# Two output tiles of a weight piece computed together, contraction tile by contraction tile

## What is computed

```python
h = rmsnorm(x)
q_a, k_a, v_a, u_pool, q_mem = split(h @ w_in)
y0 = window_attention(q_a, k_a, v_a)        # 8 heads, window of two chunks of 64, ALiBi, sinks
y1 = multiscale_pool(u_pool)                # windows 2, 4, 8, 16, then a linear map per group
y2 = memory_attention(q_mem, mem_k, mem_v)  # 4 heads of 128 into 256 memory tokens
merged = sum(sigmoid(h @ Wg_i + bg_i) * (y_i @ w_branch_i) for i in range(3))
x = x + merged @ w_out
x = x + square(relu(rmsnorm(x) @ w_up)) @ w_down
out = rmsnorm(x)
```

## Time and profile before

| | |
|---|---|
| Time, median of 3 runs | 3052.1 us (3051.82 to 3055.05) |
| Span of the profiled execution (its own time, first to last instruction) | 3050.7 us |
| TensorE busy | 3000.1 us, 98% |
| VectorE busy | 1367.5 us, 45% |
| ScalarE busy | 982.3 us, 32% |
| GpSimd busy | 194.1 us, 6% |
| HBM traffic | 96 GB/s over the span |
| Mean granted TensorE clock | 0.996 |

### The profile page before, as it was taken

One profiled execution on the slowest core, in us unless ns is written; L12 is line 12 of the kernel. 1 busy time (PEld: TensorE's weight loads), 2 busy tenths in 40 slices (PEclk: granted clock), 3 DMA queues, 4 the chain that ended last, 5 costly groups with the idle time before them and its releaser, 6 DMA issues.

```text
span 3050.7 us, 36914 instructions
## 1 busy us (share of the span) xinstructions
PE 3000.1 (98%) x14045; PEld 2468.1 (81%) x14045; DVE 1367.5 (45%) x1709; ACT 982.3 (32%) x1457; POOL 194.1 (6%) x191
## 2 busy tenths in 40 slices
PE   8999999999999999999999999999999999999998
PEld 7788888888778888888877888888887788888886
DVE  4542354444344335544435424544444532454444
ACT  4442232222344233222234423322223432332223
POOL 0100110000010111000001011100000101100000
PEclk9999999999999999999999999999999999999999
DMA  5122333322312233333231224233322122432322
GB/s 187 35 78 85 118 131 97 97 96 97 98 39 90 90 124 118 97 97 100 93 98 39 83 90 164 84 102 97 97 91 84 51 82 97 160 97 92 98 97 86
DMA packets 290351, 294.06 MB, mean 96 GB/s; under 512 B 9704, under 2 KB 285212, under 8 KB 290204
## 3 DMA queue, kind: packets, MB, share of 16 engines
q1 hardware_dynamic: 287900, 283.71, 28.8%
q0 software_dynamic: 2304, 8.39, 0.7%
HBM read 283.67 MB, written 8.39 MB: 96 GB/s over the span
## 4 chain that ended last, share of the span: by engine, by line
PE 90%; issue 5%; DVE 2%; POOL 1%; ACT 1%; DMA 0%; POOLq 0%; DVEq 0%; ACTq 0%
PE ps L979 28%; PE ps L981 27%; PE ps L980 27%; PE ps L984 2%; PE ps L1108 2%; PE ps L1109 2%; PE ps L1077 1%; POOL sq_sum L957 1%; PE ps L1135 1%; PE ps L1118 1%; ACT sq L351 0%; DVE u_lo L792 0%; DVE scores L700 0%; DVE mx L705 0%; DVE out_tm L883 0%
## 5 line engine op out<-in xcount | busy, mean ns | idle before, releaser
L979 PE MATMUL ps<-h_hi,w_hi 128*128 128x512 f32 x2240 | 884.8, 395 | 12.5 <-issue 12.5
L980 PE MATMUL ps<-h_lo,w_hi 128*128 128x512 f32 x2240 | 874.6, 390 | 0.0
L981 PE MATMUL ps<-h_hi,w_lo 128*128 128x512 f32 x2240 | 874.6, 390 | 0.0
L611 DVE TENSOR_TENSOR w_lo<-stage,w_hi 128x2048 fp32r<-128x2048 f32 (+1 forms) x269 | 559.9, 2081 | 643.2 <-ACT w_hi L351 642.0
L351 ACT ACTIVATE w_hi<-stage 128x2048 fp32r<-128x2048 f32 (+2 forms) x287 | 485.1, 1693 | 525.7 <-PE ps L981 524.5
L979 PE MATMUL ps<-u_hi,w_hi 128*128 128x512 f32 x1280 | 501.5, 392 | 5.5 <-DVE u_lo L792 5.5
L979 PEld LDWEIGHTS ps<-h_hi,w_hi 128*128 128x128 f32 x2240 | 422.1, 188 | 100.6 <-issue 14.2
L981 PE MATMUL ps<-u_hi,w_lo 128*128 128x512 f32 x1280 | 498.8, 390 | 0.0
L980 PE MATMUL ps<-u_lo,w_hi 128*128 128x512 f32 x1280 | 498.4, 389 | 0.0
L981 PEld LDWEIGHTS ps<-h_hi,w_lo 128*128 128x128 f32 x2240 | 421.9, 188 | 88.1
L980 PEld LDWEIGHTS ps<-h_lo,w_hi 128*128 128x128 f32 x2240 | 422.1, 188 | 86.4 <-issue 1.0
(11 more groups left out here) (154 smaller groups left out, 2081.9 us busy)
## 6 DMA issues: line engine op xcount, KB each, us to landing
stage<-in_w_up SPq DMA_DIRECT2D x128, 512.0 KB, 4.6
stage<-in_w_down SPq DMA_DIRECT2D x128, 512.0 KB, 4.0
stage<-in_w_gate SPq DMA_DIRECT2D x96, 512.0 KB, 4.2
stage<-in_w_in SPq DMA_DIRECT2D x60, 512.0 KB, 4.7
stage<-in_w_out SPq DMA_DIRECT2D x32, 512.0 KB, 4.1
x_tm<-in_x SPq DMA_DIRECT2D x5, 2048.0 KB, 9.5
stage<-in_w_branch_attn SPq DMA_DIRECT2D x32, 256.0 KB, 3.0
stage<-in_w_branch_pool SPq DMA_DIRECT2D x32, 256.0 KB, 3.0
```

What stands on the lines that cost most here:

```text
L611: v.tensor_tensor(w_lo[:, slot, 0:kt, :], stage[:, slot, 0:kt, :], w_hi[:, slot, 0:kt, :].bitcast(F32), ALU.subtract).then_inc(lo_done, 1)
L979: mm(dst, wh, xh, start=first, stop=False)
L980: mm(dst, wh, xl, start=False, stop=False)
L981: return mm(dst, wl, xh, start=False, stop=last)
```

## The change

A new helper, `gemm_pair`, takes both tiles of a piece: for each contraction tile k it does the three matmuls of z = 0 in one bank, and then those of z = 1 in the next bank. `piece` waits for both banks first, and then calls it. The merge loop and the MLP use it too, apart from the first up piece of a block's first chunk, which stays as it was. In the attention stage the two groups of transposes move from k = 4 and 5 of the second tile to k = 6 and 7 of the pair. Each tile still signals `tile_done` with its last matmul.

```diff
+                def gemm_pair(slot, bank, xh, xl, kt=KT, ready=None, between=None):
+
+                    for k in range(kt):
+                        if ready is not None:
+                            ready(k)
+                        if between is not None:
+                            between(k)
+                        for z in range(2):
+                            wh, wl = w_hi[:, slot, k, z * P:(z + 1) * P], w_lo[:, slot, k, z * P:(z + 1) * P]
+                            last = product(ring[:, (bank + z) % 4, :], wh, wl, xh[:, k, :], xl[:, k, :], k == 0, k == kt - 1)
+                            if k == kt - 1:
+                                last.then_inc(tile_done, 1)
+
                 def piece(n, q0, xh, xl, kt=KT, ready=None, between=None):
 
                     pe.wait_ge(lo_done, p0 + (n + 1))
                     for z in range(2):
                         q = q0 + z
                         pe.wait_ge(emptied[q % 4], e0 + q // 4)
-                        gemm(n % 2, z, q % 4, xh, xl, kt, between if z else ready)
+                    gemm_pair(n % 2, q0 % 4, xh, xl, kt, ready, between)
...
-                        f = k - 4
+                        f = k - 6
...
                         for z in range(2):
                             bank = (2 * r + z) % 4
                             pe.wait_ge(emptied[bank], ej + r // 2)
-                            gemm(r % 2, z, bank, xh, xl, kt)
+                        gemm_pair(r % 2, (2 * r) % 4, xh, xl, kt)
...
-                            for z in range(2):
+
+                            def rows_done(k):
+                                if half and i == 0:
+                                    pe.wait_ge(u_lo_done, uc + (k + 1))
+
+                            if not (first and half == i == 0):
+                                q = place(8 * half + 2 * i, last)
+                                for z in range(2):
+                                    pe.wait_ge(emptied[(q + z) % 4], ec + (q + z) // 4)
+                                gemm_pair(i % 2, q % 4, xh, xl, KT, rows_done)
+                            for z in range(2 if first and half == i == 0 else 0):
                                 t = 8 * half + 2 * i + z
```

## The result

The changed kernel takes 3204.57 us (median of 4 runs, 3202.37 to 3206.3) against 3052.3 us; the ratio with its 95% interval, from all the runs and not from the two medians, is 1.0494 (1.0479 to 1.0509). It is 4.9% slower; the forecast was 1.3%, 3092 us, and a range up to 3105. The direction was right and the size was wrong by almost four times.

What follows compares the result with a forecast made beforehand. TensorE, busy 3000.1 of 3050.7 us, was taken as the bound, so its stalls are paid in full. 32.5 + 1.8 + 1.4 + 2.7 + 2.4 - 1.0 = 39.8 us gave 3092 us, 1.3% slower, range 3080 to 3105.

Steps and rivals of the forecast that it cites:

- Item 1: Attention stage: probability copies queue behind ScalarE's late first-tile copy, TensorE loses 2.03 us in each of 16 steps, 32.5 us.
- rival (a): TensorE's clock falls in the 16 new stalls, about 1.6 us each, adding 26 us: 3118 us; chance 7%.
- Rival (a2): Clock falls inside each of the 272 pieces through pauses at bank switches, some 435 us more, 3530 us; chance 1%.
- (b): Bank alternation speeds up the matmul stream, so not slower: 40 us gain cancels the loss, 82 us gives 3010; chance 4%.
- (c): The attention stage's stall is hidden and only items 2 to 6 act: 7.3 us, 3059 us; chance 3%.
- (d): More waits than found, such as late weights in several pieces: another 10 to 25 us, 3102 to 3117; chance 8%.
- Item 2: Output projection: both banks must be empty at piece start, 0.15 us at three borders in each of 4 blocks, 1.8 us.
- Item 3: Gate piece after the pooling products: it now needs bank 1 at its start too, 0.34 us per block, 1.4 us.
- Item 4: Entry to the MLP: GpSimd's last additions, and so the token sums, come 0.68 us later per block, 2.7 us.
- Item 5: First MLP chunk's first down piece: VectorE gets two up tiles together, delaying w_lo for the second; 0.6 us, 4 times, 2.4 us.
- Item 6: Entry to the output projection: the one gain, partly filling the second u_lo wait; -0.25 us, 4 times, -1.0 us.
- The work that covers: Memory-attention stage, merge loop and up pieces: existing slack hides the late tile, costed at nothing.

Runs made afterwards that it cites:

- experiment 3: Changed kernel plus 8 extra 128x512 matmuls before TensorE's wait for the probability copies, filling the stall: 3094.68 us, 1.0135 of before.
- experiment 4: Changed kernel plus 16 extra 128x512 matmuls behind the wait for the probability copies, before the small products, in each of 16 steps: 3165.45 us, 1.0366 of before.
- experiment 6: Kernel before, unpaired, plus a TensorE wait for u_lo_done before up pieces 1 to 3 of the two middle MLP chunks, 24 stalls: 3121.39 us, 1.0217.
- experiment 1: Changed kernel, but ScalarE copies an attention-stage piece's first tile after the four probability copies: 3068.09 us, 1.0044 of before.
- experiment 5: Kernel before, unpaired, plus 4, 5 or 6 extra ScalarE copies between the halves of the probability copies: 3094.48, 3154.81 and 3194.61 us.
- experiment 8: On experiment 1, last output piece tile by tile: 3058.32 us; also output pieces 1 and 2, post-pooling gate piece, first chunk's last up piece: 3053.8 us.

## Why the prediction was wrong

**The first tile comes late, 0.68 us before the end: right.** In step 0 ScalarE's copy of it starts at 93.36, 0.64 us before TensorE is through with the piece at 94.00.

**Item 1, the attention stage.** The place, the chain and the length were right: forecast 2.03 us, measured 1.92 on average. The loss per step was not, because the sentence "Nothing of it is made up later" looked only at what the later work could gain back, not at what it could lose. The step that failed is the price of a stall in item 1: the sum counts it at its length, 2.03 us, and puts the clock behind it at nothing. It cost 1.92 + 6.9 = 8.8 us. I had the mechanism as rival (a), but gave it 7% and priced it at 1.6 us a fall. That price was from the earlier trace rows, where full-size matmuls follow. Behind this stall stand 32 products whose matmuls are small and far apart, and 20 score products; the clock stayed low over all of them, up to 17 us, and a fall cost 6.9 us (experiment 3 against the changed kernel). 16 x 6.9 = 110 us is nearly all of the 112.6 us between forecast and result. And the reason against it, "each stall follows a long dense stretch", was the wrong side to look at: experiments 4 and 6 have the same dense stretch ahead of the stall and dense work behind, and the clock falls in 1 of 16 and 5 of 24. A long stretch of sparse work alone doesn't do it either: in the kernel before and in experiment 1 the same small products run at the full clock, and so they do behind the filled stall of experiment 3. The long slow stretch takes both. The other reason, "the granted clock is 1.00 with shorter gaps", did not carry over to this place: stalls of 1.03 us in front of the small products were enough in 4 of 16 steps (experiment 5).

**Rival (a2), the clock falls with the change of banks: refuted.** In experiment 8 nearly all pieces alternate, with a mean clock of 0.995. The rule of the Trainium skill on psum-queue depth-cycling ("TensorE: Matmul & The Clock Gate") is about a TensorE that pauses between its groups; here it doesn't pause at a bank switch (1328 matmuls in 300 us), and the clock doesn't swing.

**Rivals (b), (c), (d).** The spacing is unchanged, so no gain from alternation. The stall was not hidden. There were no stalls in further places.

**Item 2** (0.15 us a border): the pieces start 12.0 us apart instead of 11.8 at two borders, 0.2 each, and the third border grew by as much. **Item 3** (0.34): 0.4. **Item 4** (0.68): 1.0 and three falls of the clock, together 9.8 us in experiment 8 for 2.7 forecast; GpSimd's two additions, now side by side with VectorE's `h_lo`, last 3.02 us instead of twice 1.34. **Item 5** (0.6): the listed wait is 0.45, and the distance grew by 0.7. **Item 6**: alone it gives 0.66 a block; in the changed kernel the entry itself starts 0.6 later, because two additions by GpSimd now overlap a `w_lo` operation (2.84 us instead of 2.33), so that nothing is left. Together these items are 14 us by experiment 1, forecast 7.3.

**A reading that was wrong.** TensorE did not wait "in any regular way only for `u_lo`". The list of the kernel before also has a wait for `out_tm` at every block's end, and three idle stretches at the block starts, 12.5 us in all:

```profile
PE ps L984 <- DVE out_tm L883: 6.5, 8, 1.4
```

In the changed kernel they are 6.5 and 12.8 us, so the forecast didn't suffer by it.

**The work that covers.** The memory-attention stage, the merge loop and the middle of the MLP took the late tile without a wait, as costed.

## What to carry to other kernels

When a change delays a buffer's completion, go through the in-order queue of its reader: what stands behind the copy in program order waits too, even if it needs nothing of it. Here moving one copy behind four others was worth 136 us.

Price a new stall of TensorE together with the work right behind it. If that is dense, a stall of 2 us cost here its length and seldom more (one of 4 us at a block's start did fell the clock each time); if it is many small matmuls, it can cost several times its length in slow clock. Filling the stall, or putting it ahead of full-size matmuls, was cheap insurance here.

When a rival has the right mechanism, take its price from a place with the same neighbours, not from the only place where the trace happens to show it.

## What the runs showed of the chip that I had not expected

A stall of 1.03 us in front of small products felled the clock in 4 of 16 cases, 1.51 us in 12, 1.99 us in 16, while 2.27 us in front of full-size matmuls did in 5 of 24. With the same stall of 1.96 us, 16 extra matmuls of 128x512 behind it made the kernel 39 us faster. The same stall of 1.17 us with the same work behind it, at the token sums, felled it in none to all four of the blocks, depending on the kernel. The slow stretches were 3.4 us long where dense work followed (6.8 at some block starts) and 10 to 17 us where the small products did. Operations of GpSimd and VectorE took longer when they ran at the same time: two additions went from 2.7 to 3.02 us, and one `h_lo` from 0.75 to 1.32. What in the small products keeps the clock low, their size or the gaps between them, was not taken apart.
